# The first down step of two MLPs as a seven-product fold, norm passes regrouped behind the border, two chunk conversions moved ahead of copies

## The reference, cut to what matters

```
h = layer_norm(DN_ALPHA * h + mix, g, b)
h = layer_norm(DN_ALPHA * h + square(relu(h @ w_up)) @ w_down, g, b)   # w_up 1024x4096, w_down 4096x1024
```

## Time and profile before

| what | value |
|---|---|
| median of 3 runs | 1810.41 us |
| the profiled execution | 1810.77 us, span 1809.0 us |
| TensorE busy | 1778.9 us, 98% |
| VectorE busy | 1274.1 us, 70% |
| ScalarE busy | 866.1 us, 48% |
| GpSimd busy | 256.2 us, 14% |

### The profile page before, as it was taken

The page is one execution under the profiler, slowest core; times in us unless marked ns, Lnnn a source line. Parts: engine busy times, 40 slices in busy tenths (PEclk is TensorE's granted clock), DMA queues, the critical chain, the costliest instruction groups (busy, mean ns, idle before and its releaser), DMA issues.

```text
span 1809.0 us, 22776 instructions
## 1 busy us (share of the span) xinstructions
PE 1778.9 (98%) x8948; PEld 1452.9 (80%) x8948; DVE 1274.1 (70%) x2068; ACT 866.1 (48%) x1348; POOL 256.2 (14%) x189
## 2 busy tenths in 40 slices
PE   8999999999999999999999999999999999999998
PEld 7775788888888888878888888888756898888886
DVE  4897566987788578467777776876767645564774
ACT  4548454454444543554444544575466453332333
POOL 0241101121210054000111111100012001110102
PEclk9999999999999999999999999999999999999999
DMA  6221404544445122141533333322202422421331
GB/s 218 64 77 35 154 24 163 186 140 140 163 163 166 47 70 70 47 137 50 187 131 126 117 116 124 100 83 93 70 25 68 131 70 70 140 78 62 117 116 47
DMA packets 120060, 189.36 MB, mean 105 GB/s; under 512 B 7800, under 2 KB 72536, under 8 KB 116880
## 3 DMA queue, kind: packets, MB, share of 16 engines
q1 hardware_dynamic: 118416, 182.81, 30.8%
q0 software_dynamic: 1392, 4.82, 0.9%
q10 hardware_dynamic: 144, 0.26, 0.0%
HBM read 185.72 MB, written 2.16 MB: 104 GB/s over the span
## 4 chain that ended last, share of the span: by engine, by line
PE 84%; DVE 10%; ACT 4%; issue 2%; DMA 0%; SPq 0%; DVEq 0%; ACTq 0%
PE bank L766 11%; PE bank L768 11%; PE bank L767 11%; PE bank L961 6%; PE bank L963 6%; PE bank L962 6%; PE bank L740 3%; PE bank L742 3%; PE bank L741 3%; PE bank L1050 2%; PE bank L1034 2%; PE bank L1025 2%; DVE gb L2746 2%; PE bank L863 2%; PE bank L864 2%
## 5 line engine op out<-in xcount | busy, mean ns | idle before, releaser
L2263 DVE TENSOR_TENSOR wl<-raw,wh 128x2048 fp32r<-128x2048 f32 (+1 forms) x163 | 360.5, 2214 | 116.6 <-ACT wh L1487 116.4
L1487 ACT ACTIVATE wh<-raw 128x2048 fp32r<-128x2048 f32 x169 | 309.0, 1837 | 255.6 <-PE bank L963 64.8
L766 PE MATMUL bank<-xh,wh 128*128 128x512 f32 (+1 forms) x872 | 340.3, 390 | 0.0
L767 PE MATMUL bank<-xh,wl 128*128 128x512 f32 (+1 forms) x872 | 340.0, 390 | 0.0
L768 PE MATMUL bank<-xl,wh 128*128 128x512 f32 (+1 forms) x872 | 340.0, 390 | 0.0
L766 PEld LDWEIGHTS bank<-xh,wh 128*128 128x128 f32 (+1 forms) x872 | 163.8, 188 | 34.9 <-issue 0.8
L768 PEld LDWEIGHTS bank<-xl,wh 128*128 128x128 f32 (+1 forms) x872 | 163.8, 188 | 34.7
L767 PEld LDWEIGHTS bank<-xh,wl 128*128 128x128 f32 (+1 forms) x872 | 163.6, 188 | 34.3
L961 PE MATMUL bank<-wh,uh 128*128 128x512 f32 x432 | 168.4, 390 | 0.0
L963 PE MATMUL bank<-wh,ul 128*128 128x512 f32 x432 | 168.1, 389 | 0.0
L962 PE MATMUL bank<-wl,uh 128*128 128x512 f32 x432 | 168.1, 389 | 0.0
(11 more groups left out here) (418 smaller groups left out, 3438.6 us busy)
## 6 DMA issues: line engine op xcount, KB each, us to landing
raw<-in_mlp_w_up SPq DMA_DIRECT2D x32, 1024.0 KB, 5.9
raw<-in_mlp_w_down SPq DMA_DIRECT2D x32, 1024.0 KB, 5.0
raw<-in_w_ada SPq DMA_DIRECT2D x24, 1024.0 KB, 5.0
raw<-in_b_w_in SPq DMA_DIRECT2D x12, 1024.0 KB, 5.2
raw<-in_w_gate SPq DMA_DIRECT2D x11, 1024.0 KB, 5.3
raw<-in_w_up SPq DMA_DIRECT2D x11, 1024.0 KB, 5.3
raw<-in_w_down SPq DMA_DIRECT2D x11, 1024.0 KB, 5.0
raw<-in_w_in SPq DMA_DIRECT2D x10, 1024.0 KB, 5.2
```

What stands on the lines that cost most here:

```text
L766: pe.matmul(o, H[:, k, c], xh[:, k, :], start=k == 0, stop=False)
L767: pe.matmul(o, L[:, k, c], xh[:, k, :], start=False, stop=False)
L1487: act.activation(slots[slot_of[i]][0][:, 0:n], raw_of(i)[:, 0:n], ACT.Copy).then_inc(*s_high.up(i))
L2263: dve.tensor_tensor(L[:, 0:n], raw_of(i)[:, 0:n], H[:, 0:n].bitcast(F), ALU.subtract).then_inc(*s_low.up(i))
```

## The change

Block 0 of both MLPs goes by `fold` too; `down_first` is gone on all engines. The norm passes 0 to 5 stand together at the head of VectorE's MLP program, 6 and 7 and the two corner differences behind the split of up(1,1)'s chunk. GpSimd does the hidden sums of block 0 before it loads the next gain. The table `HOMES` sets the slots, `ADA` spreads the ada chunks anew (same total). In the last step the last hidden split comes ahead of a chunk's split. In two places ScalarE (in one VectorE too) converts a weight chunk ahead of copies that stood in front of it.

```diff
-ADA = {0: [(0, 0, 0), (1, 0, 1), (1, 0, 1), (1, 0, 1), (1, 0, 1), (1, 0, 1), (1, 1, 1), (1, 1, 1)],
-       1: [(0, 0, 0), (1, 1, 1), (0, 0, 1), (0, 0, 1), (0, 0, 1), (0, 0, 1), (0, 0, 1), (0, 0, 0)]}
+ADA = {0: [(0, 0, 0), (1, 0, 0), (1, 0, 1), (1, 0, 1), (1, 1, 1), (1, 0, 1), (1, 1, 1), (1, 1, 1)],
+       1: [(0, 0, 0), (1, 0, 0), (0, 0, 1), (1, 0, 1), (0, 0, 1), (1, 0, 1), (0, 0, 1), (0, 0, 0)]}
+HOMES = [(2, 3, 0, 2, 3), (3, 0, 2, 3, 0), (2, 0, 3, 2, 0), (3, 0, 2, 3, 0), (2, 0, 3, 2, 0), (3, 0, 2, 3, 0), (2, 0, 3, 2, 0)]
...
+        for n in range(1, 8):
+            u0, u1, X, Y, W = HOMES[n - 1]
+            slots(u0, u1)
             plan_up(i, n)
+            plan_fold("m%d" % (i + 1), n - 1, mlp_w_down[i], (n - 1) * 512, (X, 1, Y, W), ADA[i][n][2])
+        slots(3, 2)
         plan_down(i, 7)
...
-        STEPS = {"m1": (1, 6), "m2": (1, 6), "m3": (0, 3)}
+        STEPS = {"m1": (0, 6), "m2": (0, 6), "m3": (0, 3)}
...
@@ ScalarE, mlp @@
                 for i in range(4):
                     relu(0, i // 2, i % 2)
-                    w.wait_ge(*s_act.at((key, "square", 0, i)))
-                    act.activation(UH4[:, FIRST[i], :], rb[:, i, :], ACT.Copy).then_inc(*s_xhigh.up((key, "u", 0, i)))
...
+                high_of(key, 0, P4)
+                high_of(key, 0, P1)
+                high_of(key, 0, P2)
+                for n in range(1, 8):
...
                         last_high(2)
+                        last_high(3)
                         weights(q1)
-                        last_high(3)
...
@@ ScalarE, rows of y, then q2 @@
-                        half("y", 0, GNC, None)
+                        half("y", 0, GNC, None, range(4))
+                        cur.make(high)
+                        half("y", 0, GNC, None, range(4, 8))
...
+            cur.take(high)
+            cur.take(high)
             for t in range(T):
-                if t % 2 == 0:
-                    cur.take(high)
...
@@ VectorE, mlp @@
+                for i in range(6):
                     affine(x_key, i, n_gb)
+                for s in (P4, P1, P2):
+                    low_half_of(key, 0, s)
+                for n in range(1, 8):
                     d = n - 1
                     iX, iZ, iY, iW = folds[key, d]
                     cur.take(low, 0)
                     cur.take(low, 0)
                     ada_sum()
+                    if n == 1:
+                        for i in range(6, 8):
+                            affine(x_key, i, n_gb)
+                        for t in (2, 3):
+                            corner_less(t)
                     for s in (P6, P7, P5, P3):
                         low_half_of(key, d, s)
...
                         last_low(3)
                         for t in (2, 3):
-                            corner(t, ALU.add, (key, "more", t))
+                            corner_more(t)
                         lasting(P4, 2, 0, True)
+                        weights(q1)
                         added(d, P3)
...
@@ VectorE, rows of y, then GpSimd @@
-                    for k in range(8):
+                    for k in range(4):
+                        split("y", 0, k)
+                    cur.make(low)
+                    for k in range(4, 8):
                         split("y", 0, k)
...
             load_two(ln_mix_g[0], ln_mix_b[0])
+            hidden_sums("m1", 0)
             w.wait_ge(*s_row.at(("x1", "h", T - 1)))
             load_two(ln_mlp_g[0], ln_mlp_b[0])
```

More of the change, by code:

```diff
@@ L272, in plan_mlp @@
         plan_up(i, 0)
[L273 to L280, removed]
+        for n in range(1, 8):
+            u0, u1, X, Y, W = HOMES[n - 1]
+            slots(u0, u1)
             plan_up(i, n)
-            plan_fold("m%d" % (i + 1), n - 1, mlp_w_down[i], (n - 1) * 512, (2 - own, 1, own, 3), ADA[i][n][2])
-        slots(2, 3)
+            plan_fold("m%d" % (i + 1), n - 1, mlp_w_down[i], (n - 1) * 512, (X, 1, Y, W), ADA[i][n][2])
+        slots(3, 2)
         plan_down(i, 7)
@@ L593, in freed @@
                 return s_gemm.at(("o3", T - 1, 1))
-            if key != "m3" and d == 1:
-                return s_gemm.at((key, "u read", 0)) if s in FIRST else s_gemm.at(None)
+            if d == 0 or d == 1 and s == P4:
+                return s_gemm.at(None)
             return s_gemm.at((key, "P", d - 2, s, 1)) if s == P4 else s_gemm.at((key, "P", d - 1, s, 1))
@@ L973, in fold @@
                 ada_turn()
[L975 to L991, removed]
             def mlp(key, x_key):
@@ L996, in mlp @@
                         gemm_T((key, "up", n, q), x_key)
[L997 to L1000, removed]
+                    fold(key, n - 1)
             scored = []
@@ L1654, in mlp @@
                     relu(0, i // 2, i % 2)
-                    w.wait_ge(*s_act.at((key, "square", 0, i)))
-                    act.activation(UH4[:, FIRST[i], :], rb[:, i, :], ACT.Copy).then_inc(*s_xhigh.up((key, "u", 0, i)))
-                for q in range(2):
-                    cur.take(high)
[L1659 to L1666, removed]
+                high_of(key, 0, P4)
+                high_of(key, 0, P1)
+                high_of(key, 0, P2)
+                for n in range(1, 8):
                     d = n - 1
@@ L2477, in mlp @@
             def mlp(key, x_key, n_gb):
-                last = {(t, c): ((key, "down", 0), t, c) for t in range(T) for c in range(2)}
+                last = {(t, c): (x_key, "h", t) for t in range(T) for c in range(2)}
+                scaled = set()
                 def last_low(i):
@@ L2487, in into @@
                     w.wait_ge(*s_row.at(last[t, c]))
-                    dve.tensor_tensor(hv, hv, ps, ALU.add).then_inc(*s_row.up(name, ((key, "down", 6), t, c)))
+                    if (t, c) in scaled:
+                        dve.tensor_tensor(hv, hv, ps, ALU.add).then_inc(*s_row.up(name, ((key, "down", 6), t, c)))
+                    else:
+                        dve.scalar_tensor_tensor(hv, hv, ALPHA, ps, ALU.mult, ALU.add).then_inc(*s_row.up(name, ((key, "down", 6), t, c)))
+                    scaled.add((t, c))
                     last[t, c] = name
@@ L2508, in lasting, with corner_less, corner_more @@
                             banks.read[where] = s_row.at(name)
-                def corner(t, op, name):
-                    hv = h[:, t, 512:1024]
+                def corner_less(t):
+                    hv, name = h[:, t, 512:1024], (key, "less", t)
+                    w.wait_ge(*s_row.at(last[t, 0]))
+                    dve.tensor_tensor(hv, hv, h[:, t, 0:512], ALU.subtract).then_inc(*s_row.up(name))
+                    last[t, 1] = name
+                def corner_more(t):
+                    hv, name = h[:, t, 512:1024], (key, "more", t)
                     w.wait_ge(*s_row.at(last[t, 0]))
                     w.wait_ge(*s_row.at(last[t, 1]))
-                    dve.tensor_tensor(hv, hv, h[:, t, 0:512], op).then_inc(*s_row.up(name, ((key, "down", 6), t, 1)))
+                    dve.scalar_tensor_tensor(hv, hv, ALPHA, h[:, t, 0:512], ALU.mult, ALU.add).then_inc(
+                        *s_row.up(name, ((key, "down", 6), t, 1)))
+                    scaled.add((t, 1))
                     last[t, 1] = name
[L2518 to L2525, removed]
                 def owed():
@@ L3479, in gpsimd_program @@
             load_two(ln_mix_g[1], ln_mix_b[1])
+            hidden_sums("m2", 0)
             w.wait_ge(*s_row.at(("x3", "h", T - 1)))
```

5 lines of the change are left out of this document (1 added, 4 removed).

## The result

The changed kernel takes 1814.97 us (median of 13 runs, 1811.59 to 1816.51), the kernel before beside it 1810.49 (13 runs, 1809.45 to 1812.64): ratio 1.0022, 95% interval [1.0015, 1.0029], slower by 4.0 us with 2.7 to 5.3. On another chip it was 1815.33 against 1810.27, ratio 1.0023 [1.0014, 1.0032]. The forecast was 1811.1 with a range to 1814.7. The stall that it forecast is in the trace, link by link; a cost that comes with the stall was not in the sum.

The account below looks back on a forecast made before the run. TensorE, busy 98% of 1809.0 us, was taken as the bound. Two MLPs at 3.7 + 0.1 - 2.7 gave +2.2, the chunk moves -1.5: +0.7 on the 1810.41 median, 1811.1 us, with 8 in 10 for 1804.5 to 1814.7.

Parts of the forecast that it names:

- The stall that it forecast: First fold of each MLP: TensorE waits about 3.7 us at P6, the third product, for VectorE's split and P1's addition.
- Price and saving: Down step on TensorE: 96 matmuls become 84 at 0.2267 us each, saving 2.72 us per MLP, 5.44 for both.
- VectorE's series: VectorE's work up to P1's addition: ends at 294.2, or 297.4 with GpSimd's sums, while TensorE wants P6 at 293.6.
- the bounds 0 and 1.1 for the norm passes: Cost of each norm pass meeting a GpSimd sum, which no row showed; 1.1 us taken, P6 wait 1.5 without it.
- The second stall: Rival: up(2,0) behind the first fold waits 1.1 to 2.2 us more per MLP; 1814.9 us, chance 0.17.
- the chain from the fourth product to P7's addition: Behind the first stall: conversion, split, ada product, one sum wait and addition, 8.1 us, before up(2,0) needs the bank.
- the margin of 0.1 us: At up(2,0): 8.1 us of chain against TensorE's arrival after 8.16 us; 0.1 to spare, a further meeting costs 1.1.
- The two chunks: Two weight chunks converted ahead of copies remove TensorE waits of 1.12 and 0.51 us; together -1.5 us.
- The term of 1.1 in front of the second MLP: Second output chunk before 791.59: earlier ScalarE conversion removes TensorE's idle; gain 1.1 us, bounds 0 and 1.12.
- that of q2: Split before 1199.88, its conversion behind two copies: moving it 1.0 us earlier gains 0.4 us, bounds 0 and 0.51.
- the sum per MLP: Net per MLP: P6 stall 3.7, plus 0.1 behind it, less 2.7 of saved matmuls; +2.2 for both MLPs.
- The range: 8 in 10 for 1804.5 to 1814.7 us, taking in most of the rival that cover holds and the second stall's price.

Follow-up runs that it names:

- late_norm_best: late_norm with one ada chunk of the first MLP moved from up step 2 to up step 3; 1804.82 us, ratio 0.9966 to the kernel before.
- ada_off_step1: Changed kernel with the ada chunk of up step 1 moved to up step 3 in both MLPs, norm passes left; 1812.21 us, ratio 1.0.
- late_norm: Changed kernel with norm passes 6, 7 and two corner subtractions per MLP moved behind the additions of P6; 1809.98 us, ratio 0.9994.
- chunks_only: Kernel before plus the two weight-chunk moves alone, without the fold in the first step; 1808.3 us, ratio 0.9986.
- fold_only: Changed kernel less the two weight-chunk moves, seven-product first step kept; 1816.63 us, ratio 1.0033.

## Why the prediction was right, and where not

- **Price and saving.** 12 matmuls x 0.2267 per MLP: 2.7 us in the accounts of both MLPs. late_norm_best has most of it: in its profile the second MLP is 2.4 us shorter than before, the first 0.8, with waits of 0.2 at P6, 0.5 at 538 and 0.2 at 559 (2.0 shorter in the three kernels built from it, whose first MLP is the same). By the times it gains 5.9 to 6.2 us, where fold and chunk moves without any stall would give 7.5 to 8.
- **VectorE's series.** Forecast: ada product +1.04, norm passes +1.1 each, P1's first addition done at 297.4, P6 waits 3.7. Measured: 2.32 for 1.28, 2.27 each for 1.24, done at 297.0 (296.28 + 0.68), idle 3.6. Right, and shown by taking pieces out: corners -1.2, norm passes and corners -3.2 with 0.4 left (of 5.8 taken out, as said above). The value chosen between the bounds 0 and 1.1 for the norm passes was the upper one, by the row of another split, and that was right.
- **The rule that a VectorE instruction with two SBUF inputs is blocked by a GpSimd instruction that reads SBUF** (the Trainium skill, "SBUF — State Buffer", section "Who interferes with whom"): the trace of after agrees, with 2.27 us for the norm pass, and ada_off_step1 with 2.38 for two corner subtractions. Additions from PSUM beside the sums stay at 0.6 each.
- **The second stall** did not come in the changed kernel, where TensorE resumed late and the chain behind it had room. It came in late_norm, by the same chain. I had put the chain from the fourth product to P7's addition at 8.1 us with one wait for a sum; in the changed kernel it meets none and takes 7.2 (304.5 to 311.7). In late_norm it takes 11.1: 1.5 for the moved instructions in front of the split, 1.5 and 1.0 for the sums. So the margin of 0.1 us held with room to spare, and what used it up was put there by late_norm itself.
- **The two chunks.** Forecast 1.5, measured 2.3 to 2.5 by the times (the interval leaves 0.9 to 4.2), 2.1 by the trace of chunks_only. The term of 1.1 in front of the second MLP was 1.4, that of q2 was sized at 0.4 and was 0.8: the whole of each wait and a little behind it.
- **The step that failed is the sum per MLP: "3.7 + 0.1 - 2.7 = +1.1".** It prices an idle time by its length. Measured is 3.6 + 2.1 - 2.7 = 3.0 per MLP in fold_only, 6.0 for both instead of 2.2, and less the chunks' 2.1 to 2.5 that is 3.5 to 3.9, near the 4.0 of the changed kernel. The missing term is the granted clock, 0.50 to 0.72 in the windows with slow matmuls, of which 7 to 13 stand behind each idle time of 3.4 us and more. The trace of before shows at 617 us that the clock can fall in the middle of the kernel; around the change it has no idle time of this length to price it from, and I read the clock only in the windows there. That the time still came out 3 to 4 us from the forecast is partly luck: a price per stall 2 us too low, times two, was set off in part by chunk moves that gave 0.6 to 1.0 more than I said.
- **The range** reached up to 1814.7 by way of the second stall. The median of 1814.97 lies 0.3 us beyond it; the ratio times the 1810.41 that I had counted from gives 1814.4, just inside. The reason for its upper end was another than the one that took effect, so it held by luck.

## What to carry to other kernels

Lay out the series of the engine that feeds TensorE against the deadline of each product, and put work without a deadline behind the deadline, not ahead of it: the same 1304 us of VectorE's work, four instructions later and one ada product elsewhere, made 0.2% slower into 0.3% faster. Price a TensorE stall of 3.4 us and more, in kernels like these, at some 1.6 times its length (1.5 to 1.8 in the profiles here). When a stall is taken away, ask which chain had lived on its slack, and what the moved instructions now stand in front of: the next stall sat 13 us behind.

## What the hardware showed that was not expected

The clock behind an idle time is not the same each time. Start to start of the idle place, and slow matmuls (0.38 to 0.48 apart) counted behind it, over all profiles, at P6 and the head of up step 2: with 3.6 to 3.9 us 7, 8, 13, 7, 12, 7, 7, 7 (none without); with 2.2 to 3.0 us 0, 7, 6, 0, 0, 8; with 1.7 us 0, with 1.1 us 0. Behind the eight products of 16 rows near 617 us, over thirteen profiles, that of before first: 8, 0, 5, 6, 9, 9, 0, 8, 0, 7, 5, 6, 0. That is one place of the program with the same work right ahead of it, and it goes from 0 to 9; the stretch from the end of the first MLP to the output product takes 184.6 us with 0 of them, 185.8 to 186.0 with 5 to 8, and 187 with 9. So part of the spread of every kernel's runs, of before's too, may come from there, which is argued, not shown. The slow stretch also need not begin with the first matmul: 1.5 us behind it at 891.11, 1.1 us at 1010.62.

A VectorE pass of one SBUF input, 128x1024 times a constant, took 0.72 us, a norm pass of two inputs of the same size 1.22. The Trainium skill ("VectorE: DVE Perf Modes", section "Mode 2×_2P — use both read ports for one tensor") has it that an instruction with one tensor can stream it over both ports; the runs agree, and so did a row of before, 1.28 us for 128x2048.
